# A zero fill and a replicated table written in eight parts, one per step of the first FFN, in a two-block float32 kernel

## The reference, cut to what matters

```python
def first_block(x, ...):                      # first FFN, mixer, second FFN
    x = x + 0.5 * swiglu(rms_norm(x, ffn1_norm), w_gate, w_up, w_down)   # 1024 -> 2816 -> 1024
    ...
def second_block(x, c, w_mod, b_mod, ...):
    mod = silu(c) @ w_mod + b_mod             # 1024 x 6144: six vectors that shift, scale and gate
    sh1, sc1, g1, sh2, sc2, g2 = split(mod, 6)
    h = rms(x, norm1_w) * (1 + sc1) + sh1
    u, q, k, v = split(h @ w_in)
    y_ssm = s5(u, ...)                        # a diagonal state space layer, done here in chunks of 8 tokens
    y_attn = swa_sink(q, k, v, rel_bias, sinks)   # logits + rel_bias[bucket(distance)], window of 128 tokens
    ...
```

## Time and profile before

| | |
|---|---|
| median of three runs | 1930.44 us |
| the profiled execution | 1928.16 us |
| its span, first to last instruction | 1926.5 us |
| PE busy | 1828.4 us (95% of the span) |
| DVE busy | 1030.0 us (53%) |
| ACT busy | 718.7 us (37%) |
| POOL busy | 161.8 us (8%) |
| mean granted clock of TensorE | 0.976 |
| bytes moved by DMA | 206.77 MB, 107 GB/s over the span |

### The profile page before, as it was taken

The page is one execution under the profiler, slowest core; times in us unless marked ns, Lnnn a source line. Parts: engine busy times, 40 slices in busy tenths (PEclk is TensorE's granted clock), DMA queues, the critical chain, the costliest instruction groups (busy, mean ns, idle before and its releaser), DMA issues.

```text
span 1926.5 us, 23418 instructions
## 1 busy us (share of the span) xinstructions
PE 1828.4 (95%) x8801; PEld 1455.9 (76%) x8801; DVE 1030.0 (53%) x1436; ACT 718.7 (37%) x1005; POOL 161.8 (8%) x218
## 2 busy tenths in 40 slices
PE   7399999999999999999999999999878999999998
PEld 5288888886888677787788778888765778888887
DVE  4355633635555556654878733335655565555433
ACT  3122222223334686622323222223237254555322
POOL 2112100201000000003411020100000300000000
PEclk9699999999999999999999999999989999999999
DMA  7655522233222112122555452334120222222222
GB/s 202 195 174 174 174 91 73 94 106 122 88 88 88 66 45 66 66 88 89 184 170 163 132 162 68 99 108 175 39 116 23 66 81 93 87 95 90 74 91 86
DMA packets 171451, 206.77 MB, mean 107 GB/s; under 512 B 18140, under 2 KB 149786, under 8 KB 170866
## 3 DMA queue, kind: packets, MB, share of 16 engines
q1 hardware_dynamic: 144994, 161.97, 25.5%
q0 software_dynamic: 12400, 38.55, 6.4%
q10 hardware_dynamic: 13984, 5.27, 1.2%
HBM read 190.29 MB, written 17.56 MB: 108 GB/s over the span
## 4 chain that ended last, share of the span: by engine, by line
PE 91%; DVE 3%; DMA 3%; ACT 2%; issue 1%; POOL 0%; DVEq 0%; POOLq 0%; ACTq 0%
PE bank L1813 40%; PE bank L1777 34%; PE bank L2028 6%; DMA mod_raw<-in_w_mod 3%; PE bank L1745 2%; PE bank L1935 1%; PE bank L2052 1%; PE bank L1792 1%; PE bank L2063 0%; DVE w_lo L1074 0%; PE bank L2185 0%; PE bank L1833 0%; PE bank L1864 0%; PE bank L2131 0%; PE bank L2217 0%
## 5 line engine op out<-in xcount | busy, mean ns | idle before, releaser
L638 ACT CAST w_hi<-w_raw 128x2048 fp32r<-128x2048 f32 x158 | 301.2, 1907 | 874.4 <-PE bank L1813 446.2
L1074 DVE TENSOR_TENSOR w_lo<-w_raw,w_hi 128x2048 fp32r<-128x2048 f32 x157 | 370.4, 2359 | 463.6 <-ACT w_hi L638 463.4
L1813 PE MATMUL bank<-h_hi,w_hi 128*128 128x512 f32 x1088 | 436.2, 401 | 13.9 <-ACT h_hi L662 8.9
L1813 PE MATMUL bank<-h_hi,w_lo 128*128 128x512 f32 x1088 | 433.0, 398 | 0.0
L1813 PE MATMUL bank<-h_lo,w_hi 128*128 128x512 f32 x1088 | 344.5, 398 | 0.0
L1813 PEld LDWEIGHTS bank<-h_hi,w_hi 128*128 128x128 f32 x1088 | 206.4, 190 | 66.6 <-issue 17.3
L1813 PEld LDWEIGHTS bank<-h_lo,w_hi 128*128 128x128 f32 x1088 | 205.9, 189 | 50.2 <-DVE h_lo L1100 0.4
L1813 PEld LDWEIGHTS bank<-h_hi,w_lo 128*128 128x128 f32 x1088 | 206.9, 190 | 48.6 <-issue 0.2
L1777 PE MATMUL bank<-hid_hi,w_hi 128*128 128x512 f32 x528 | 208.9, 396 | 0.0
L1777 PE MATMUL bank<-hid_lo,w_hi 128*128 128x512 f32 x528 | 208.9, 396 | 0.0
L1777 PE MATMUL bank<-hid_hi,w_lo 128*128 128x512 f32 x528 | 208.9, 396 | 0.0
(11 more groups left out here) (405 smaller groups left out, 2360.2 us busy)
## 6 DMA issues: line engine op xcount, KB each, us to landing
w_raw<-in_w_in SPq DMA_DIRECT2D x29, 1024.0 KB, 5.2
mod_raw<-in_w_mod POOLq DMA_DIRECT2D x96, 256.0 KB, 3.5
w_raw<-in_ffn_w_gate SPq DMA_DIRECT2D x22, 1024.0 KB, 6.4
w_raw<-in_ffn_w_up SPq DMA_DIRECT2D x22, 1024.0 KB, 5.4
w_raw<-in_w_up SPq DMA_DIRECT2D x22, 1024.0 KB, 5.0
w_raw<-in_ffn_w_down SPq DMA_DIRECT2D x16, 768.0 KB, 4.2
w_raw<-in_ffn_w_down SPq DMA_DIRECT2D x16, 640.0 KB, 3.9
w_raw<-in_w_out SPq DMA_DIRECT2D x8, 1024.0 KB, 4.8
```

What stands on the lines that cost most here:

```text
L638: act.copy(w_hi[i % 2][:], w_raw[i % 2][:]).then_inc(S("w_hi_done"), 1)
L1074: dve.tensor_tensor(w_lo[s][:], w_raw[s][:], w_hi[s][:].bitcast(F32), ALU.subtract).then_inc(S("w_split"), 1)
L1813: mm = pe.matmul(bank[:], w[:, k, at], h[:, k, :], start=k == first and part == 0 and i == 0, stop=k == last and part == 1)
```

## The change

The replicated band and the zero fill are no longer two whole transfers ahead of the modulation's loads. The tile `zero` becomes 128x1088, and the function `tables(i)`, called by `beside("ffn1", tables)` behind the eight loads of step i, stores one eighth of the zeros (128 runs of 4352 bytes) and 16 of the band's 128 copies (8x16 runs of 1532 bytes). The tile `band_row` moves from tile 11 to tile 19 of its area, past hidden tiles that the eight steps write. ACT's wait for the band moves from ahead of step 0 to ahead of step 8, beside that for the zeros; all waits count eight parts.

```diff
+ZEROS = CHUNK * SHIFT * 2 * NS * SG // (P * BESIDE_STEPS)
...
-            (10, "rel", [33, NQ], F32), (11, "band_row", [NQ, BAND], F32),
-            (BESIDE, "zero", [P, T], F32),
+            (10, "rel", [33, NQ], F32), (BESIDE + 3, "band_row", [NQ, BAND], F32),
+            (BESIDE, "zero", [P, ZEROS], F32),
...
-            def beside(name):
+            def beside(name, behind=None):
...
                         pool.wait_ge(S("mod_step"), i * MOD_STEPS + (first * MOD_STEPS + k + 1))
                         pool.dma_start(mod_raw[:, k % MOD_SLOTS, :], wm[:, k, bass.ds(i * T + first * T, T)])\
                             .then_inc(S(f"mod_landed{k % MOD_SLOTS}"), 16)
+                    if behind:
+                        behind(i)
...
             pool.wait_ge(S("band_made"), 1)
-            pool.dma_start(band_dram.ap(), band[:].unsqueeze(1).to_broadcast([NQ, P, BAND])).then_inc(S("band_stored"), 16)
             done(pool.memset(zero[:], 0.0))
-            flat = tz_dram.rearrange("h s t c -> (h s t c)").rearrange("(p r c) -> p r c", p=P, c=T)
-            pool.dma_start(flat, zero[:].unsqueeze(1).to_broadcast([P, CHUNK * SHIFT * 2 * NS * SG // (P * T), T])).then_inc(S("zero_stored"), 16)
-            beside("ffn1")
+            flat = tz_dram.rearrange("h s t c -> (h s t c)").rearrange("(p c) -> p c", p=P)
+            copies = P // BESIDE_STEPS
+
+            def tables(i):
+
+                pool.dma_start(flat[:, bass.ds(i * ZEROS, ZEROS)], zero[:]).then_inc(S("zero_stored"), 16)
+                pool.dma_start(band_dram.ap()[:, bass.ds(i * copies, copies), :],
+                               band[:].unsqueeze(1).to_broadcast([NQ, copies, BAND])).then_inc(S("band_stored"), 16)
+
+            beside("ffn1", tables)
...
-            pool.wait_ge(S("band_stored"), 16)
+            pool.wait_ge(S("band_stored"), 16 * BESIDE_STEPS)
...
                         if name == "ffn1":
-                            act.wait_ge(S("zero_stored"), 16)
+                            act.wait_ge(S("zero_stored"), 16 * BESIDE_STEPS)
+                            act.wait_ge(S("band_stored"), 16 * BESIDE_STEPS)
...
                     if extra == MOD_END:
-                        act.wait_ge(S("zero_stored"), 16)
+                        act.wait_ge(S("zero_stored"), 16 * BESIDE_STEPS)
...
-            act.wait_ge(S("band_stored"), 16)
             swiglu("ffn1")
```

## The result

| | before | changed |
|---|---|---|
| median | 1930.31 us (4 runs, 1929.10 to 1930.57) | 1893.03 us (4 runs, 1892.09 to 1894.46) |
| profiled execution | 1928.16 us | 1894.46 us |
| its span | 1926.5 us | 1892.9 us |
| granted clock, mean | 0.976 | 0.982 |

The ratio is 0.9812 with a 95% interval of 0.9801 to 0.9824: the changed kernel is 1.9% faster. The medians differ by 37.3 us, the two profiled executions by 33.7.

A forecast was written before the change was run, and what follows sets the result against it. PE was taken to set the end, with a hole while loads waited behind two stores. Removing 33.5 us of idle time and 1.9 of slow products gives 1930.44 - 35.4 = 1895.1 us, range 1893 to 1900.

The forecast's parts named there:

- The mechanism: Two stores at the head of POOL's queue delay the first modulation loads, leaving PE idle 31.98 us after step 0.
- The sum: Step 2 starts at 74.00 us instead of 109.37: 35.4 us gained, 33.5 of idle time and 1.9 of slow products.
- The signs named beforehand: No PE idle in step 0, step 2 near 74.0 us, clock 1.00 from 30 us, DMA share near 0.67, steps 23.3 us.
- Step 0's margin: The gate panel's `w_lo` is ready at 47.78 or 49.50 us, PE wants it at 50.71: 2.9 or 1.2 us spare.
- Rival A: Step 0 becomes the tight place: late loads make PE wait 1 to 9 us, 1899 to 1900 or up to 1904; chance 0.10.
- What the parts cost: Sixteen small stores in steps 0 to 7: POOL 1.5 us a step, DMA share 0.53 to about 0.67, nothing on the path.
- so the band and the zeros took 407: Of 549 engine-us on POOL's queue from 20 to 84 us, 12 loads took 142 and the two stores 407.
- the 4 us taken from it: DMA time of one step's two parts, taken near 4 us because half the engines do the slow part; range 3.2 to 10.5.
- the bound of 10.5 us: Upper bound for one step's two parts: an eighth of each landing time without overlap, 36.3/8 + 47.6/8.
- Rival B: Step 1's gate panel on SP's queue was not held by the stores: only 12.7 us gained, 1917.7 us; chance 0.03.
- Rival C: Parts do not shrink with size, so each step's first loads come late: slower from about 25 us a step; chance 0.03.
- The noise: Three runs shown lie within 0.4 us; 2 us allowed for the rest, giving the forecast its own range 1893 to 1897.

The follow-up runs named there:

- the repeat: The changed kernel run again with no edit, beside the kernel before: 1892.99 us, median of five, ratio 0.9816.

## Why the prediction was right

The range 1893 to 1900 holds the measured 1893.03 at its very edge, 2.1 us below the forecast of 1895.1. The mechanism came out as stated; that the number fell inside is luck, since the repeat has its median at 1892.99, just outside.

- **The sum** (33.5 us of idle time, 1.9 of slow products) came out as worked out: step 2 starts at 74.00 us. The chain after it is PE alone, as before. The signs named beforehand held in the main: no idle time of PE in step 0, steps of 23.29 us. The clock was 0.98 from 30 to 50 us and not 1.00, and the DMA share 0.84 in step 1 and not near 0.67.
- **Step 0's margin** was put at 1.2 to 2.9 us and is 2.1. Three terms were off: DVE starts at 36.77 instead of 36.16, since it waits for ACT's silu of `c`, which the long wait had hidden and the prediction left out; from k = 0 to k = 4 it takes 4.42 us instead of 5.12; and from there to the end of `w_lo` 7.43 instead of 6.50. Together they make 0.84 us, 48.62 against 47.78. Rival A did not happen, but a wait of 4.35 us for one load does it, as the parts between the loads showed.
- **What the parts cost** is nothing: POOL 1.4 us (1.5 taken), DMA share 0.70 from step 2 on (0.67), all inside the idle time named.
- **Why the stores were slow**: the step that failed is "so the band and the zeros took 407. One eighth is 51 engine-us: 3.2 us if spread evenly", with the 4 us taken from it. The total is near (33 x 8 + 11 x 16 = 440), but more than half of it is the band's, and a store from 8 rows goes to eight engines: a step's two parts are 4.1 + 1.4 = 5.5 us of those eight. It did not matter here, because the bound of 10.5 us was covered too. Four parts a step came out 33 us above what the even spread gave. The whole band was expected on eight engines, but at 26 us of them where it takes 33, and landed at 35.7; that expectation was 10 us too low.
- **Rival B** was dismissed rightly: the panel was held by the stores, as the whole stores on ACT's queue and behind step 7 show. But the reason given, that 43.7 us "speak against even turns", was a wrong reading. The two queues took even turns by packets (580 and 578), and the rule that the prediction cites from the Trainium skill ("DMA: Bandwidth & Descriptors", section "Queues, rings and completion order"), turns of one packet at a time, agrees with that count. A panel in packets of 1 KB is held because each of its turns costs it a slow packet of 4 to 4.6 KB.
- **Rival C** (slower by a longer queue time per step) had its point at 25 us of queue time a step. The test with four times the stores comes near to that case: steps of 31.6 us and 1952.64, slower than before.
- **The noise** was set too low: "the three runs shown lie within 0.4 us" hid a spread of 5 us of the kernel before (1926.37 to 1931.73 in nine runs). The 37.3 us of the first comparison and the 35.9 of the second are the same gain.

None of the versions tried beats the changed kernel beyond the noise (the parts stored twice, at 1892.15, are level with it); PE has no wait left in the steps concerned.

## What to carry to other kernels

When an engine waits for a small load, look at what stands ahead of it on its queue and at what else the DMA engines are doing: here two stores that nothing read before the second block held everything for 48 us. Cutting them into parts small enough for the slack of a loop's step, and placing each behind the step's own loads, costs nothing while the DMA engines still have time in the step; moving them whole behind the first step's loads only moved the wait. Count a transfer's cost on the engines that it uses, with the rate that a trace shows for its form, and not by its bytes: 1.5 MB from 8 rows cost 23 us, the same from 16 rows 8, 4.4 MB from 128 rows 6.

## What the runs showed of the hardware that was not expected

- A store of 128 copies of 8 rows of 1532 bytes went out at 46 to 49 GB/s with half of the DMA engines busy; the stretch with a fill of 2048-byte runs from 128 rows moved 408 GB/s with all of them, SP's panels included. From 16 rows the first landed in 18.7 us instead of 35.7; a pitch of 1536 bytes changed nothing (35.6).
- POOL's and SP's queues took even turns by packets and not by bytes (580 packets of 4.0 KB and 578 of 1.0 KB in the same 14 us). So a panel on a queue of its own took 43.7 us beside the stores, not much less than the 47.65 of a load behind them.
- After a stall of 4.6 us, the same 48 products took 13.72 us in one profile of the changed kernel and 12.97 in another (clock 0.92 and 0.94 over 14 us). Single executions differ by 3.6 us (changed) and 5.4 us (before) in all, and the longer ones have the lower mean clock.
